# Hybrid decoder layer on one core: input order of the second MLP matrix, earlier head loads, head work ahead of residual sums, running retention states

## What is computed

```python
def step(R, qkv):                       # retention, chunks of 128 tokens, 8 heads
    qc, kc, vc = qkv
    inner = jnp.einsum('bhcd,bhed->bhce', qc, kc) * dmask[None]
    o = (jnp.einsum('bhce,bhed->bhcd', inner, vc)
         + jnp.einsum('bhcd,bhde->bhce', qc, R) * xi[None, :, :, None])
    R = (R * chunk_decay[None, :, None, None]
         + jnp.einsum('bhcd,bhce->bhde', kc * zeta[None, :, :, None], vc))
    return R, o
...
ro = _layer_norm_noaffine(ro).astype(x.dtype).reshape(B, L, RET_W)
y_ret = jax.nn.silu(rg) * (ro * ret_beta)
...
mix = jnp.concatenate([y_ret, y_dsa], axis=-1) @ w_out
x = x + gate1[:, None, :] * mix
h = _modulate(_rms_norm(x, norm2_g), shift2, scale2)
y = jnp.square(jax.nn.relu(h @ w_mlp1)) @ w_mlp2
return x + gate2[:, None, :] * y
```

## Time and profile before

| | us |
|---|---|
| median of 3 runs | 2454.93 |
| lowest, highest | 2454.20, 2455.87 |
| profiled execution | 2454.89 |
| its span on the core | 2452.4 |
| PE busy in the span | 2383.3 |
| DVE, ACT, POOL busy | 982.2, 641.3, 973.6 |
| mean granted clock, share of full speed | 0.986 |

### The profile page before, as it was taken

One profiled execution on the slowest core, in us unless ns is written; L12 is line 12 of the kernel. 1 busy time (PEld: TensorE's weight loads), 2 busy tenths in 40 slices (PEclk: granted clock), 3 DMA queues, 4 the chain that ended last, 5 costly groups with the idle time before them and its releaser, 6 DMA issues.

```text
span 2452.4 us, 26881 instructions
## 1 busy us (share of the span) xinstructions
PE 2383.3 (97%) x10926; PEld 1933.9 (79%) x10926; DVE 982.2 (40%) x1349; ACT 641.3 (26%) x894; POOL 973.6 (40%) x414
## 2 busy tenths in 40 slices
PE   5999998999999899899999999999999999999999
PEld 3677687788878788788888888888888888888887
DVE  2236899777744576742122022031131221221121
ACT  4222332223223221232222122232232221221231
POOL 1233244234433234444444444444444444444442
PEclk8999999999999999999999999999999999999999
DMA  9875465667822731322322333223322223322331
GB/s 353 327 284 193 152 219 191 206 227 271 291 86 91 235 121 69 103 69 103 103 86 87 103 103 102 80 92 103 103 103 79 92 103 103 103 77 94 103 122 50
DMA packets 183649, 342.14 MB, mean 140 GB/s; under 512 B 4337, under 2 KB 31124, under 8 KB 182804
## 3 DMA queue, kind: packets, MB, share of 16 engines
q1 hardware_dynamic: 174944, 336.77, 40.1%
q10 hardware_dynamic: 8628, 4.28, 0.6%
HBM read 324.26 MB, written 16.78 MB: 139 GB/s over the span
## 4 chain that ended last, share of the span: by engine, by line
PE 87%; DVE 8%; DMA 2%; issue 1%; SPq 1%; ACT 1%; POOL 0%; ACTq 0%; DVEq 0%
PE pj L1177 51%; PE pa L1177 30%; DVE part_rows L999 1%; DVE score L924 1%; DVE m L923 1%; PE pa L1181 1%; DMA ada_first<-w_ada_in 1%; PE pa L1249 1%; DVE sq L1153 1%; PE pa L1368 1%; DMA raw<-w_in_in 1%; DMA resid<-xT_dram 1%; DVE ada_acc L999 1%; PE pa L1402 1%; PE pa L1425 1%
## 5 line engine op out<-in xcount | busy, mean ns | idle before, releaser
L724 POOL TENSOR_TENSOR w_lo<-raw,w_hi 128x1024 fp32r<-128x1024 f32 (+1 forms) x396 | 955.1, 2413 | 1412.4 <-ACT w_hi L494 1412.4
L494 ACT ACTIVATE w_hi<-raw 128x1024 fp32r<-128x1024 f32 (+1 forms) x396 | 417.1, 1054 | 1540.9 <-PE pj L1177 1000.7
L1177 PE MATMUL pj<-h,w_hi 128*128 128x512 f32 x1664 | 520.3, 394 | 3.7 <-DVE h L819 2.5
L1177 PE MATMUL pj<-w_hi,h 128*128 128x512 f32 (+1 forms) x1536 | 484.2, 392 | 16.4 <-DVE rot L951 9.9
L1177 PEld LDWEIGHTS pj<-h,w_hi 128*128 128x128 f32 x1664 | 312.5, 190 | 74.6 <-issue 9.3
L1153 DVE TENSOR_TENSOR sq<-relu 128x512 f32<-128x512 f32 x64 | 160.5, 2508 | 515.9 <-ACT relu L680 515.9
L1177 PEld LDWEIGHTS pj<-w_hi,h 128*128 128x128 f32 x1536 | 289.1, 191 | 88.8 <-issue 24.7
L1177 PE MATMUL pa<-h,w_hi 128*128 128x512 f32 x1152 | 357.0, 391 | 0.0
L1177 PE MATMUL pj<-h,w_lo 128*128 128x512 f32 x832 | 325.8, 392 | 0.0
L1177 PE MATMUL pj<-mid,w_hi 128*128 128x512 f32 x1024 | 317.8, 391 | 5.6 <-DVE mid L1157 5.6
L1177 PE MATMUL pa<-mid,w_hi 128*128 128x512 f32 x1024 | 316.0, 390 | 0.0
(11 more groups left out here) (165 smaller groups left out, 1694.3 us busy)
## 6 DMA issues: line engine op xcount, KB each, us to landing
raw<-w_mlp_in SPq DMA_DIRECT2D x64, 2048.0 KB, 8.9
ada_rows<-w_ada_in SPq DMA_DIRECT2D x64, 1024.0 KB, 5.2
raw<-w_in_in SPq DMA_DIRECT2D x22, 2048.0 KB, 10.2
ada_first<-w_ada_in SPq DMA_DIRECT2D x32, 1024.0 KB, 9.6
raw<-w_out_in SPq DMA_DIRECT2D x8, 2048.0 KB, 8.7
ret<-ret_dram SPq DMA_DIRECT2D x32, 256.0 KB, 4.3
raw<-w_in_in SPq DMA_DIRECT2D x4, 1792.0 KB, 14.4
x_nat<-x_in SPq DMA_DIRECT2D x4, 1024.0 KB, 10.1
```

The costliest lines, as they stand in the source:

```text
L494: act.activation(split_chunk(w_hi, u, j), raw_chunk(u, j), ACT.Copy).then_inc(hi_done, 1)
L724: pool.tensor_tensor(split_chunk(w_lo, u, j), raw_chunk(u, j), split_chunk(w_hi, u, j).bitcast(F32), ALU.subtract).then_inc(lo_done, 1)
L1177: last = pe.matmul(dst, lhs[a], rhs[b], start=start and n == 0, stop=stop and n == 2)
```

## The change

- Second MLP matrix: output tiles 0 and 1 are computed together. First the tiles 0 to 6 of `mid` for output tile 0, then the same for output tile 1, then tile 7 for each (`second_first`). The waits for `mid_ready` 1 to 7 stay with output tile 0, the eighth stands behind output tile 1's first seven. Both weight buffers come free at the end. In the last step the transposes of the finished output tiles 0 and 1 both follow chunk 2.
- Head loads: head 0 in slot `Q_HEAD` = 93 (as soon as the last of the conditioning sums is taken), head 1 in slot 106 (when the last head of attention has been taken), both ahead of the last store. Head 2 stays behind the store and now waits until the store has landed, and so does ACT before it copies the first transposes, which overlay `nat`.
- Head work ahead of residual sums: on DVE `add_out(r - 1)` now stands at the end of slot `r`.
- Running states: PE computes each of the three products of keys and values once, and DVE makes the sums: copy, add, add, each waiting for the one before.

```diff
@@ sync engine @@
             def load_head(k):
-                if k < 3:
+                if k == 0:
+                    sp.wait_ge(mod_taken, 8 + ADA_SUMS)
+                elif k == 1:
                     sp.wait_ge(y_ready, HEADS)
-                    sp.wait_ge(mod_taken, 8 + ADA_SUMS)
+                elif k == 2:
+                    sp.wait_ge(nat_stored, 64)
                 else:
                     sp.wait_ge(z_ready, k - 2)
...
+                    if q == Q_HEAD:
+                        load_head(0)
+                    if g == KV - 1 and r == 38:
+                        load_head(1)
                     if r == 39:
                         store_nat(3, g, v_taken, 4 * g + 4)
...
                 if u == U_WO - 1:
-                    for k in range(3):
-                        load_head(k)
+                    load_head(2)
@@ scalar engine @@
+                if q == Q_WO:
+                    act.wait_ge(nat_stored, 64)
@@ vector engine @@
             def ret_state(k):
                 dve.wait_ge(state_done, k + 1)
-                dve.tensor_copy(state[:].rearrange("p a b -> p (a b)"), pa[:, 2, 0:3 * P]).then_inc(state_ready, 1)
+                own.link(dve.tensor_copy(state[:, 0, :], pa[:, 2, 0:P]))
+                own.link(dve.tensor_tensor(state[:, 1, :], pa[:, 2, P:2 * P], state[:, 0, :], ALU.add))
+                dve.tensor_tensor(state[:, 2, :], pa[:, 2, 2 * P:3 * P], state[:, 1, :], ALU.add).then_inc(state_ready, 1)
...
             for r in range(16):
-                add_out(r, False)
                 k, odd = divmod(r, 2)
...
+                if r > 0:
+                    add_out(r - 1, False)
             ret_norm(7)
             ret_low(7)
-            for r in range(16, 32):
-                add_out(r, True)
+            for r in range(15, 32):
+                add_out(r, r >= 16)
@@ tensor engine @@
-                for n in range(1, NB):
-                    for e in range(n):
-                        last = pe.matmul(pa[:, 2, P * (n - 1):P * n], ret[:, k % 3, 2, e, :], ret[:, k % 3, 3, e, :],
-                                         start=e == 0, stop=e == n - 1)
+                for n in range(NB - 1):
+                    last = pe.matmul(pa[:, 2, P * n:P * n + P], ret[:, k % 3, 2, n, :], ret[:, k % 3, 3, n, :],
+                                     start=True, stop=True)
...
+            def second_first(c):
+
+                for kks in (range(7), (7,)):
+                    for j in range(2):
+                        if kks[0] == 0:
+                            pe.wait_ge(relu_done, j + 1 + 8 * c)
+                            pe.wait_ge(lo_done, 4 * (U_MLP + 4) + j + 1 + 32 * c)
+                        for kk in kks:
+                            if j == 0:
+                                pe.wait_ge(mid_ready, kk + 1 + 8 * c)
+                            last = product(pj[:, j, :], [w[:, j, P * kk:P * kk + P] for w in (w_hi, w_lo)],
+                                           [mid[:, kk, s, :] for s in (HI, LO)], kk == 0, kk == 7)
+                        if kks[-1] == 7:
+                            last.then_inc(chunk_used, 1)
...
+                second_first(c)
                 for v in range(4):
                     banks = pa if v % 2 else pj
-                    for j in range(4):
+                    for j in range(2 if v == 0 else 0, 4):
...
-                        if final and 4 * v + j > 0:
+                        if final and v == 0 and j == 2:
+                            output(0)
+                        if final:
                             output(4 * v + j - 1)
```

More of the change, by code:

```diff
@@ L94 @@
               for n in range(ADA_SUMS)]
+Q_HEAD = max(ADA_SUM_AT) + 2
 ADA_EARLY = [n for n in range(ADA_PIECES) if n % 2 and ADA_AT[n] < Q_LOOP + Q_TURN_AT - 1]
@@ L1570, in mlp_step @@
                         for kk in range(8):
-                            if v == 0 and j == 0:
-                                pe.wait_ge(mid_ready, kk + 1 + 8 * c)
                             last = product(banks[:, j, :], [w[:, j, P * kk:P * kk + P] for w in (w_hi, w_lo)],
```

## The result

The changed kernel took 2437.39 us (median of 5 runs, 2431.11 to 2445.19), the kernel before 2455.87 us in the same set (median of 5, 2454.2 to 2458.02): a ratio of 0.993, 95% interval 0.9912 to 0.9948. The forecast was 2436.7 us, 18.2 us less; 16.1 to 18.5 us were measured. Both kernels spread by more than 10 us in one set or another, so the two profiled executions of the changed kernel are read stretch by stretch, cut at marks that each trace has. The fourth mark is the start of the second matrix behind its first wait; the fifth the same in the eighth step. All numbers are us.

A forecast was written before the change was run, and what follows sets the result against it. PE's matmuls were taken to bound the kernel; 13.3 (first heads) + 4.0 (other six heads) + 0.9 (MLP loop) = 18.2 us off 2454.93 us gave 2436.7 us, with an 8-in-10 range of 2433.5 to 2442.5.

The forecast's parts named there:

- What bounds the kernel: Whole kernel: PE's matmuls fill nearly all of the chain, so only fewer matmuls or fewer PE gaps change the time.
- Second MLP matrix: MLP loop: only the eighth tile's wait goes, 0.1 us per step, 0.9 us in all; bounds 0 and 8.9 us.
- Running states: Output projection heads: PE drops 3 of 6 products, 0.67 us per head, 4.0 us in six; DVE's 1.0 us stays hidden.
- Head loads: Start of output projection: the 4.36 us load gap and its slow work go; residual issued about 802.9, landing at 817.9.
- Order on DVE, simulation of the first heads: First heads: no wait for `innerT`, PE waits 1.3 us for z, chunk 4 starts at 824.7 instead of 838.04: 13.3 us.
- my range: First heads: 2434 to 2441 us for residual landings between 816 and 820, where a gap over 3 us begins slow work.
- The residual did come sooner: Output projection rival: residual lands no sooner, at 822.9, leaving a 6.3 us gap; gain 10.9 us, 2444.0 us; chance 0.11.
- The whole wait: MLP loop rival: all waiting for `mid` goes, 8.9 us instead of 0.9, giving 2428.7 us; chance 0.05.
- DVE isn't the bound in the heads: Heads rival: DVE becomes the bound if three state instructions take over 1.9 us, giving 2443 us; chance 0.03.
- Output tile 0's weights weren't late: MLP loop rival: weights come late because the buffer is held 4.8 us longer, losing 38 us, 2475 us; chance 0.03.

The follow-up runs named there:

- Six tiles first: The changed kernel with both output tiles taken over six input tiles first and the last two afterwards: 2430.56 us, ratio 0.9888 to the kernel before.
- DVE order alone: The kernel before with nothing but the residual sum of a chunk one slot later on DVE: 2447.78 us, ratio 0.9967.
- the MLP order alone: The kernel before with nothing but the new order of the second matrix's first two output tiles: 2453.63 us, ratio 0.9997.
- the one with 24 products: The changed kernel with 24 unused one-column fp32 products (96 PE instructions) added at its start: 2438.05 us, ratio 0.9929 to the kernel before.

## Why the prediction was right, and where it was wrong

- **What bounds the kernel** held: PE alone. Each part moved the end by what it took from PE's gaps or matmuls, and they add up to 17.3 of 17.55 us.
- **Second MLP matrix.** Right in which wait goes: 0.12 us per step alone, 0.1 forecast. Six tiles first shows the other end of the bounds, 1.1 us per step, and that the seventh tile held it. What I left out of the sum is the loop's code. In the changed kernel the term of +0.9 us became -0.3 in the first profile (-0.47 + 0.14) and +0.5 in the second. Nothing in the rows of before shows such a fetch, and I never asked what the shorter code ahead of the loop does to the loop.
- **Running states.** 0.71 us per steady head for 0.67; six heads gave 4.23 us alone and 4.25 in the second profile, for 4.0. DVE's three dependent instructions took 0.94 us (800.22 to 801.16), the estimate was 1.0. The row's 0.112 us per record decided rightly: 12 records took 1.34 us and 6 take 0.67. The 56 ns that the Trainium skill (TensorE: Matmul & The Clock Gate, section on the back-to-back issue gap) gives would have made it 0.34 us per head, half of what was measured.
- **Head loads.** The gap of 4.36 us and its slow work went. The store landed in 4.15 us for the 5.4 that I took, and four issues took 3.39 us for 2.0; the two errors cancel, and the residual's issue came 7.67 us behind the store for the forecast's 7.6 (and 7.22 and 6.29 in others). The store lands in 4.1 to 4.2 us where nothing is issued right behind it, as in the changed kernel, and in 5.0 to 5.5 us where loads follow at once, as in the row of before. The Trainium skill (DMA: Bandwidth & Descriptors, section on the anatomy of one DMA), by whose figures 4.4 us is the estimate for the store, was nearer than that row. The sum on the residual started 23.39 us behind the store in one profile and 22.46 in the other, for the forecast's 22.7.
- **Order on DVE, simulation of the first heads.** This is the term that was mis-sized in the first profile: 9.3 us for 13.3. The forecast had z ready 28.1 us behind the store's issue (823.4 - 795.33); it was 30.8. Of the 2.7 us, 0.7 are the residual's and 2.0 POOL's split, during which z's multiply took 2.71 us for 0.69. The forecast took DVE's tail behind the sum at its length in the kernel before and never asked what POOL does at that moment. The gap of 4.20 us then brought the slow work that I had expected from such a gap but not forecast here: 0.95 us up to chunk 4 and 0.64 in it. In the second profile the simulation holds to 0.2 us: 29.56 for 29.4. That it met the split in one profile and not in the other hung on 0.9 us of the residual's landing, so which of the two a run shows is luck. The residual alone can bring the gap to 1.92 us with slow work behind it (six tiles first), which my range had put at 3 us.
- **Rivals.** The residual did come sooner, by 4.3 us and 5.2. The whole wait didn't go. DVE isn't the bound in the heads. Output tile 0's weights weren't late: steps of 175.07 us.
- **The number.** 2436.7 us against 2437.39 and 2438.18. Its closeness in the first execution is partly luck: 4.1 us in the first 790 us covered what the first heads lacked. In the second, 17.55 of 18.2 us arrived, with the mechanism as forecast but for the loop's code.

What could have been seen ahead: in the kernel before the squares of the MLP, a multiply of 128x512 like z's, take 2.5 us each, where z's took 0.69 us. The page's group, kernel before (busy us, mean ns, idle):

```profile
L1153 DVE TENSOR_TENSOR sq<-relu 128x512 f32<-128x512 f32 x64 | 160.5, 2508 | 515.9 <-ACT relu L680 515.9
```

They do in the changed kernel too. POOL and then DVE ahead of its second matrix:

```profile
1110.15 2.39 POOL L733 TENSOR_TENSOR w_lo<-raw,w_hi 128x1024 fp32r<-128x1024 f32 x1 [3.05 <-ACT w_hi L501]
```

```profile
1110.59 2.51 DVE L1165 TENSOR_TENSOR sq<-relu 128x512 f32<-128x512 f32 x1 [2.33 <-ACT relu L689]
```

The square ends at 1113.10, 0.56 us behind the split. The square stands ahead of the seventh tile's low part on DVE, and the 1.8 us that it takes beyond 0.69 are more than the 1.0 us by which that tile is late. So a split at another moment should remove the wait for `mid` at its source; that is argued from the rows and wasn't tried.

## What to carry to other kernels

Cut a noisy span at marks that both kernels share and sum the stretches: here a start-up that varies by 11 us hid, and in one execution repaid, an error of 4 us. When work is taken from DVE's queue, look at what POOL does at the new moment, not only at the length of the row that moves. And a wait behind a pipeline of tiles is best moved by as many tiles as are late: one tile up gave 0.12 us a step, two tiles up 1.1.

## What the runs showed of the hardware

- **DVE behind POOL.** DVE's gate sum, gate product, squares and z's multiply, which read SBUF alone, end 0.3 to 0.6 us after POOL's subtraction when they start during it: 0.43 us became 2.20, 0.69 became 1.82, 2.51 and 2.71. When z's multiply started 0.09 us ahead of the subtraction, it kept its 0.69 us. The sum on the residual, with an operand in PSUM, kept its 0.75 us (DVE order alone, at 826.85, within POOL's 826.17 to 828.84). The Trainium skill has this: by the page SBUF — State Buffer, section "Who interferes with whom", DVE and GpSimd share a port pair, and whichever starts first holds it for its whole instruction; a DVE instruction needs it if it has two SBUF inputs or runs in a two-port mode. The rows of the gate product, the squares and z's multiply agree; that the gate sum, with one input, runs in such a mode isn't shown by any row.
- **Where a loop's code lies counts.** 96 instructions fewer ahead of the loop, and 45 more packets of 16 KB came, with 0.05 to 0.4 us lost at the loop's start in two to five of the seven steps; 96 put back, and none of these came. The Trainium skill (Runtime: NRT & Kernel Launch, section "Instruction fetch mechanics") says that code comes in blocks of 16 KiB and that a taken branch outside the current window of two blocks forces a fetch. The packets' size agrees. But in the kernel before, in the MLP order alone and in the one with 24 products the loop of 768 matmuls and as many weight loads goes back every 175 us, and not one such packet came between 1459 and 1810 us: here the page's rule and the measurement differ, and a loop can stay in place. How many blocks stay isn't shown, nor why 96 instructions decide it.
- **The clock in the first 200 us.** The granted clock there was 0.88 to 0.92 over 14 profiles of work that is alike but for the 24 products in two of them, and the last store's issue came between 791.27 and 802.25 us.
- **A short gap can be enough.** Behind 1.92 us without matmuls the granted clock was 0.57 in the window from 824 to 828 us (six tiles first); behind 1.26 us it was 1.00 in the same window (changed kernel, second profile). That is one execution each.
